# Dilated attention with the even tokens ahead of the odd ones, and value products of two pairs together

## What is computed

```
DIL_PATTERNS = ((128, 1), (512, 4), (2048, 16));  DIL_HEADS = 4;  HEAD_DIM = 64
for g, (w, r) in enumerate(DIL_PATTERNS):        # queries see keys at 0, +-r, ..., +-w/2
    o, lse = banded_attention(strided(q), strided(k), strided(v), w // (2 * r), 64, slopes[4g:4g+4], r)
wts = softmax(stack(lses), axis=0)               # over the three patterns of a head slot
out = sum(wts * outs)
```

## Time and profile before

| | us |
|---|---|
| median of 3 runs | 3207.03 (3205.33 to 3211.16) |
| profiled execution | 3205.56, span 3203.7 |
| TensorE busy / weight loads busy | 2553.3 (80%) / 1314.0 (41%) |
| VectorE, ScalarE, GpSimd busy | 1359.4, 881.3, 583.8 |
| DMA, mean over the span | 344 GB/s |

### The profile page before, as it was taken

The page is one execution under the profiler, slowest core; times in us unless marked ns, Lnnn a source line. Parts: engine busy times, 40 slices in busy tenths (PEclk is TensorE's granted clock), DMA queues, the critical chain, the costliest instruction groups (busy, mean ns, idle before and its releaser), DMA issues.

```text
span 3203.7 us, 31231 instructions
## 1 busy us (share of the span) xinstructions
PE 2553.3 (80%) x10802; PEld 1314.0 (41%) x10802; DVE 1359.4 (42%) x3265; ACT 881.3 (28%) x2329; POOL 583.8 (18%) x557
## 2 busy tenths in 40 slices
PE   8998766656999875666598887789897989977776
PEld 6775311111777521122165642245462544523222
DVE  0352100001144200000244767777867687677774
ACT  1231000000122101000123334455633475343433
POOL 0000000000000000000001334433434344344442
PEclk9999877787999887788899999999999999999999
DMA  7324899999533299999911899999999999999997
GB/s 287 127 103 155 341 428 428 428 428 428 209 121 132 105 422 427 428 427 428 423 74 63 340 422 421 421 421 402 419 422 421 410 414 408 420 421 422 421 421 317
DMA packets 120188, 1101.86 MB, mean 344 GB/s; under 512 B 13376, under 2 KB 17248, under 8 KB 20960
## 3 DMA queue, kind: packets, MB, share of 16 engines
q1 hardware_dynamic: 44576, 559.83, 42.1%
q0 software_dynamic: 73728, 536.90, 40.4%
q10 hardware_dynamic: 1728, 3.14, 0.3%
HBM read 1095.64 MB, written 4.19 MB: 343 GB/s over the span
## 4 chain that ended last, share of the span: by engine, by line
PE 42%; DMA 41%; DVE 9%; ACT 4%; issue 3%; POOL 0%; SPq 0%; DVEq 0%; ACTq 0%; POOLq 0%
PE ps L619 23%; DMA wbuf<-in_puv,ar 18%; PE ps L1173 9%; DMA wbuf<-in_w_expert_up 8%; DMA wbuf<-in_w_expert_down 8%; DMA wbuf<-in_w_expert_gate 4%; PE ps L847 4%; DVE ar L1841 3%; ACT ar L1890 2%; PE ps L719 2%; PE ps L623 2%; DMA wbuf<-in_w_mem_kv 2%; PE ps L705 1%; ACT L1890 1%; DMA Y<-in_mem 1%
## 5 line engine op out<-in xcount | busy, mean ns | idle before, releaser
L1173 PE MATMUL ps<-wbuf,ar 128*128 128x512 f32 x2048 | 968.2, 611 | 217.5 <-ACT ar L1890 217.3
L1841 DVE CUSTOM_DVE_ANT_0 ar<-wbuf,Y 128x1024 f32<-128x1024 f32 x512 | 627.4, 1225 | 334.8 <-DMA wbuf<-in_puv,ar 326.0
L847 PE MATMUL ps<-wbuf,ar 128*32 128x512 f32 x3072 | 495.0, 783 | 316.1 <-DMA wbuf<-in_w_expert_up 133.7
L2367 POOL DMA_INDIRECT wbuf<-in_puv,ar x512 | 558.7, 1091 | 842.5 <-PE ps L1173 804.8
L1173 PEld LDWEIGHTS ps<-wbuf,ar 128*128 128x128 f32 x2048 | 368.2, 192 | 769.8 <-issue 768.0
L619 PE MATMUL ps<-HT,wbuf 128*128 128x256 f32 (+2 forms) x2784 | 500.1, 339 | 12.5 <-DMA wbuf<-in_w_mem_kv 4.5
L619 PEld LDWEIGHTS ps<-HT,wbuf 128*128 128x128 f32 (+1 forms) x2784 | 439.2, 192 | 71.8 <-issue 14.1
L1890 ACT ACTIVATE ar<-ar 128x1 f32<-128x1 f32 (+2 forms) x1052 | 270.1, 257 | 657.6 <-DVE ar L1841 629.8
L847 PEld LDWEIGHTS ps<-wbuf,ar 128*32 128x32 f32 x3072 | 99.4, 127 | 699.0 <-issue 205.7
L2351 POOL TENSOR_TENSOR sm<-sm,co 128x1 f32<-128x1 f32 (+1 forms) x17 | 10.7, 632 | 1689.1 <-DVE sm L1208 1355.3
L1887 ACT COPY ar<-ps 128x512 f32<-128x512 f32 (+2 forms) x131 | 72.0, 550 | 620.4 <-PE ps L847 307.2
(11 more groups left out here) (139 smaller groups left out, 1506.9 us busy)
## 6 DMA issues: line engine op xcount, KB each, us to landing
wbuf<-in_w_expert_gate SPq DMA_DIRECT2D x64, 2048.0 KB, 26.3
wbuf<-in_w_expert_up SPq DMA_DIRECT2D x64, 2048.0 KB, 26.2
wbuf<-in_w_expert_down SPq DMA_DIRECT2D x64, 2048.0 KB, 27.3
wbuf<-in_w_in SPq DMA_DIRECT2D x22, 2048.0 KB, 11.2
wbuf<-in_peer_w_q SPq DMA_DIRECT2D x12, 2048.0 KB
wbuf<-in_w_o SPq DMA_DIRECT2D x6, 2048.0 KB, 7.1
wbuf<-in_b_w_in SPq DMA_DIRECT2D x6, 2048.0 KB
wbuf<-in_w_branch_b SPq DMA_DIRECT2D x4, 2048.0 KB, 15.3
```

The lines of the kernel that those rows point to most:

```text
L847: m = T.e.matmul(ps(jobs[n])[32 * k:32 * k + 32, :], lhs(c, k), v[:, k, 512 * n:512 * n + 512], start=(c == 0), stop=(c == 7), tile_positi ...
L1173: m = T.e.matmul(acc[n][:, :], DG[:, j % 4, :], rows_of(name)[:, 1024 + 512 * n:1536 + 512 * n], start=(j == 0), stop=(j == 127))
L1841: V.did(V.e.tensor_tensor_reduce(JK, rows_of(f"g{l}{i}.{j}")[:, 0:1024], Y[:, i, :], 1.0, 0.0, ALU.mult, ALU.add, DT[:, i, j:j + 1]), f"do ...
L2367: G.land(G.e.indirect_dma_start(out=rows_of(name), out_offset=None, in_=I["puv"], in_offset=bass.IndirectOffsetOnAxis(ap=IX[:, i, j:j + 1] ...
```

## The change

Queries and keys of the dilated attention are written with the 128 even tokens ahead of the 128 odd ones: the six jobs stream HT through a view `HE` whose innermost step is two elements (kind "E"), and the values' jobs load it as stationary operand with that step (kind "M", `proj_M`). A query block is now the tokens of one parity. The wide sub-heads see only keys of their own parity, so their scores have 128 columns each in place of 256; the local one keeps 256. A unit has 512 columns of scores, four transposes, and tables of 768 columns for 1152. Value products of a wide sub-head run per query block, over one block of keys. They are issued for two pairs at a time, after units 3 and 7, in turns on the two column halves. There are four buffers of transposed probabilities in place of two. The output is copied back to the order of tokens by a write with step two (`OAE`). Both wide sub-heads of a slot now lie on the other half of the rows than the local one.

```
+        OAE = OAT.rearrange("p c (t e) -> p c e t", e=2)
+        pb_dil = [arv(7680 + 1024 * k, 8704 + 1024 * k) for k in range(4)]
+        HE = HT[:, :, :].rearrange("p c (t e) -> p c e t", e=2)
 ...
-                    jobs.append((f"q{c}", j, "T", a, QK[:, c:c + 2, :], 0.125 if c < 6 else 1.0))
+                    jobs.append((f"q{c}", j, "E", a, QK[:, c:c + 2, :], 0.125 if c < 6 else 1.0))
-                jobs.append((f"va{i}", 3, "N", (i, 0, 512), VA[:, i, 0:512], 1.0))
+                jobs.append((f"va{i}", 3, "M", (i, 0, 512), VA[:, i, 0:512], 1.0))
 ...
         def dil_units(l):
+                local, *wide = heads = [4 * g + s for g in range(3)]
+                pv = [(f"m{l}.oa{s // 2}", 64 * (s % 2), 0, 256, k, 0, VA[:, k, 64 * local:64 * local + 64], k == 0, False)
+                      for k in range(2)]
+                for x, h in enumerate(wide):
+                    for i in range(2):
+                        pv.append((f"m{l}.oa{s // 2}", 64 * (s % 2), 128 * i, 128, 2 + x, i,
+                                   VA[:, i, 64 * h:64 * h + 64], False, (x, i) == (1, 1)))
+                pvs.append(pv)
 ...
-                        "scores": [(0, 0, 256, *qk[0]), (1, 0, 256, *qk[2]), (0, 256, 256, *qk[1])],
+                        "scores": [(0, 0, 256, q[0], kk[0]), (1, 0, 128, q[1], kk[1][:, qs]), (1, 128, 128, q[2], kk[2][:, qs])],
-                                  "parts": [(0, 0, 512, tab[:, 0:2, off:off + 256], 0),
-                                            (1, 0, 256, tab[:, 2, off:off + 256], 512)],
-                                  "cols": (0, 768), ...
+                                  "parts": [(0, 0, 256, tab[:, 256 * i:256 * i + 256], 0), (1, 0, 256, tab[:, 512:768], 256)],
+                                  "cols": (0, 512), ...
+                if s % 2:
+                    us[-1]["pv"] = [(*x, p) for both in zip(*pvs[s - 1:]) for x, p in zip(both, (s - 1, s))]
+                    us[-1]["close"] = [f"m{l}.oa{s // 2}"]
 ...
+            def proj_M(job, v, e, c0, n, *names):
+                b = take(job)
+                T.did(mm(b[:, 0:n], [(HE[:, c, e, :], v[:, c, c0:c0 + n]) for c in range(v.shape[1])]), job, *names)
 ...
-                                if u["pair"] > 1:
-                                    V.wait_ge(*at[f"{p}.pv{u['pair'] - 2}"])
+                                if u["before"] >= 0:
+                                    V.wait_ge(*at[f"{p}.pv{u['before']}"])
 ...
-                        copy(OAT[:, 0, :], ps(f"{p}oa0")[:, 0:256], f"{p}oa0.out")
+                        copy(OAE[:, 0, :, :], two(ps(f"{p}oa0")[:, 0:256]), f"{p}oa0.out")
 ...
-                u["tb"], u["pb"] = tbuf[k % len(tbuf)], pbuf[u["pair"] % 2]
+                u["tb"], u["pb"], u["before"] = tbuf[k % len(tbuf)], pbuf[u["pair"] % len(pbuf)], u["pair"] - len(pbuf)
 ...
-    order = [h ^ 1 if h // 4 == 1 else h for h in range(12)]
+    order = [h ^ 1 if h > 3 else h for h in range(12)]
```

More of the change, by code:

```diff
@@ L247, in dil_units @@
                     n = 2 * s + i
-                    tab = cbuf[:, s % 2, 0:1152].rearrange("p (g n) -> p g n", g=3)
+                    tab = cbuf[:, s % 2, 0:768]
                     us.append({
-                        "scores": [(0, 0, 256, *qk[0]), (1, 0, 256, *qk[2]), (0, 256, 256, *qk[1])],
+                        "scores": [(0, 0, 256, q[0], kk[0]), (1, 0, 128, q[1], kk[1][:, qs]), (1, 128, 128, q[2], kk[2][:, qs])],
                         "soft": [{"m": mx[:, n:n + 1], "nm": nm[:, n:n + 1], "den": den_dil[:, n:n + 1],
-                                  "parts": [(0, 0, 512, tab[:, 0:2, off:off + 256], 0),
-                                            (1, 0, 256, tab[:, 2, off:off + 256], 512)],
[L254 to L260, removed]
@@ new lines, in dil_units @@
+                                  "parts": [(0, 0, 256, tab[:, 256 * i:256 * i + 256], 0), (1, 0, 256, tab[:, 512:768], 256)],
+                                  "cols": (0, 512), "tab": f"m{l}.cd{s}", "over": f"m{l}.cd{s}.used" if i else None}],
+                        "m": mx[:, n:n + 1], "nm": nm[:, n:n + 1], "den": den_dil[:, n:n + 1],
+                        "blk": [128 * b for b in range(4)], "to": range(4), "nb": 4, "pair": s, "i": i, "ni": 2,
+                        "pv": [], "close": []})
@@ L652, in chunks @@
             def chunks(v, a, rhs):
-                return [(k, [(v[:, c, 128 * (a + k):128 * (a + k) + 128], rhs[:, c, :]) for c in range(v.shape[1])])
+                return [(k, [(v[:, c, 128 * (a + k):128 * (a + k) + 128], rhs[:, c]) for c in range(v.shape[1])])
                         for k in range(2)]
@@ L695, in attend @@
                     if j >= 0 and units[j]["pv"]:
[L696 to L700, removed]
+                        pairs = sorted({x[-1] for x in units[j]["pv"]})
+                        pb = {u["pair"]: u["pb"] for u in units[:j + 1]}
+                        for jj in range(j + 1):
+                            if units[jj]["pair"] in pairs:
+                                for c in range(0, len(units[jj]["blk"]), 4):
+                                    T.wait_ge(*at[f"{p}.t{jj}.{c}.out"])
+                        for job, po, c0, w, b, i0, v, start, stop, pair in units[j]["pv"]:
                             if job not in opened:
@@ L704, in attend @@
                             a = 128 * (units[j]["ni"] * b + i0)
-                            m = T.e.matmul(ps(job)[po:po + 64, c0:c0 + w], v, units[j]["pb"][:, a:a + w],
+                            m = T.e.matmul(ps(job)[po:po + 64, c0:c0 + w], v, pb[pair][:, a:a + w],
                                            start=start, stop=stop, tile_position=(0, po))
-                        T.did(m, f"{p}.pv{pair}", *units[j]["close"])
+                        T.did(m, *(f"{p}.pv{pair}" for pair in pairs), *units[j]["close"])
                         for job in units[j]["close"]:
@@ L725, in project @@
                     done = [f"m{l}.w{w}.used"] if n + 1 == len(jobs) or jobs[n + 1][1] != w else []
-                    if kind == "T":
-                        proj_T(f"m{l}.{job}", v, x, *done)
+                    if kind in "TE":
+                        proj_T(f"m{l}.{job}", v, x, *done, rhs=HE if kind == "E" else HT)
+                    elif kind == "M":
+                        proj_M(f"m{l}.{job}", v, *x, *done)
                     else:
@@ L1992, in mixer @@
                 A.wait_ge(*at[f"{p}oa1"])
-                copy(OAT[:, 1, :], ps(f"{p}oa1")[:, 0:256], f"{p}oa1.out")
+                copy(OAE[:, 1, :, :], two(ps(f"{p}oa1")[:, 0:256]), f"{p}oa1.out")
                 def heads_b(j):
@@ L2469, in _constants @@
     put("nhalf", -0.5)
[L2470 removed]
+    return {"cd": cd, "cw": cw.reshape(4, 128, 1536), "oh": oh, "co": co}
 def _arrays(inputs):
```

41 lines of the change are left out of this document (23 added, 18 removed).

## The result

The changed kernel took 3183.84 us (median of 4 runs, 3182.91 to 3187.18) against 3206.37 for the kernel before beside it (median of 4, 3205.33 to 3211.16): a ratio of 0.9931, 95% interval 0.9918 to 0.9944, 22.5 us less. The forecast was 3184.7. The profiled execution took 3187.18 us (span 3185.4), 18.4 us less than the profiled one of before.

The account below looks back on a forecast made before the run. TensorE was taken to pace the mixers, weight transfers the experts. Per layer 2.7 + 1.8 + 6.8 - 0.15 = 11.15 us, 22.3 for two, gave a median of 3184.7 us (forecast's own range 3180 to 3192; 8 in 10: 3179 to 3196).

Parts of the forecast that it names:

- scores: Dilated attention, each unit's score products: 1.06 us falls to 0.72, saving 2.7 us a layer (1.7 to 3.4).
- Transposes: Dilated attention: six per unit become four, saving 0.22 us for each of 8 units, 1.8 us a layer.
- Value products: Dilated attention: two pairs fall from 5.46 to 2.05 us by turns on column halves, saving 6.8 us a layer.
- Waits: Tail of the dilated attention: TensorE's idle gaps sum to 2.55 us against 2.38, losing 0.15 us a layer.
- the price of the stepped operand: Query and key projections streaming every second column: no cost taken; at half rate 41.7 us more a layer.
- my own sign: Projections: records above 0.22 us would prove the forecast wrong by rival (a) or (b).
- rival (a): Query and key projections: stepped stream is slow, gain eaten from 58 ns more a record, 3268 at half rate; chance 0.12.
- the weight loads of the values: Value projections loading the stepped operand as weights: no cost taken; at half rate 5.1 us a layer.
- The clock: Attention tail: layer 0 had lost 1.5 us to a lower granted clock; same loss taken once, 1.5 either way.
- rival d: Expert stages: the weight transfers do not start sooner, so the gain is hidden; chance 0.02.
- Rival (c): Value products: turns give nothing, 128-column products bound by weight loads; saving 2.7 a layer, total 3193; chance 0.04.
- (b): Value projections: only the stepped weight loads are slow, 5.1 us a layer, total 3195; chance 0.04.

Follow-up runs that it names:

- one-run step: Changed kernel, query and key projections reading 256 columns at step two in one run across two feature blocks (wrong values): 3184.59 us.
- the repeat: The changed kernel itself, unaltered, timed and profiled again beside its variants: 3185.06 us, ratio 0.9933 to the kernel before.
- evacuation variant: Changed kernel with queries and keys streamed without a step, the even/odd reordering done by the evacuations instead: 3182.63 us, ratio 0.9928.
- untwined order: Changed kernel with the first pair's value products all ahead of the second's, so not in turns on the column halves: 3192.24 us, ratio 0.9960.
- the step of four: Changed kernel with the query and key projections' streamed operand at a step of four columns, in four runs of 64: 3272.11 us.
- the best one: Changed kernel with the reordering moved into the evacuations and side work stretched into the attention's tail: 3174.11 us, ratio 0.9899 to the kernel before.

## Why the prediction was right

**Right in the mechanism of the attention; that the median came within 1 us is luck in part.** The forecast had 11.15 us a layer, from the attention alone. In the trace the attention gave 12.0 and 10.4, together 22.4, and the projections took 4.0 and 3.6 back. Term by term, a layer: scores 0.64 us a unit where I took 0.72, so 3.4 us for 2.7, the upper end of my bounds: the two products of 128 columns fit wholly beside the one of 256. Transposes 0.21 to 0.22 a unit (six in 0.71, four in 0.49 to 0.50, beside side work), as counted. Value products 1.89 us a group where I took 2.05: 7.1 for 6.8. Waits 2.60 us of idle gaps for 2.38 before, by the three places named (1.46, 0.32 and 0.82 for 1.5, 0.35 and 0.71). The sum of these is 12.1 a layer. The bounds of the recorded terms add up to 28 us for two layers at the top, where the prediction says 26; nothing hangs on it.

**The step that failed is the price of the stepped operand.** I took nothing, on the ground that a pass takes one column in two periods of the clock and so leaves the reads slack; it is 10.8 ns a record, 2.1 us a layer. By my own sign, records above 0.22 us, rival (a) came true in a mild form, at 0.228. The breakeven that I gave for it, 58 ns, stands five times higher, so the forecast survived. For the weight loads of the values, to take nothing was right: 0.196 for 0.190, beside passes of 0.217, and the stage still takes 20.8. Without the clock's part, the attention gives 12.0 a layer (58.3, as from 83.44 to 141.73 in the one-run step, for 70.3) and the step takes 2.1 of it, 19.8 in all; the loss of 1.5 us in layer 0's tail of the kernel before, if it isn't met again, makes it 21.3 for the 22.3 of the forecast. That run, which has the changed kernel's work and no slow stretch in its mixers, is 19.3 ahead at the start of the second block.

**The clock went against it, by more than I allowed.** I took the same 1.5 us once. In both profiles of the changed kernel the tail is slow in both layers, 1.5 to 1.7 us each, and both projections start slowly, 1.5 to 1.9 us. That is why the mixers' gain in the trace is 15.6 and not the forecast's 22.3. The profiled executions (3187.18, 3189.28) are the longest of their series, but the slow stretches are not shown to be the reason: the one-run step had none of them and took 3184.59, where 3187.2 less 6.6 would be 3180.6. So of the 22.5 us of the median, and of the 21.1 of the repeat (3206.14 less 3185.06), the rows account for about 15 in the profiled executions and for 19 to 21 without slow stretches. The rest comes from the identical second block and from the spread of the runs, and it happened to fill the gap to the forecast.

**The saving reached the end** (rival d): -8.6 at the first expert product is -9.0 when the next layer begins, and -15.6 in layer 1 is -14.7 behind its experts. The products themselves come later than forecast, at 324.65 for 322 and 15.6 earlier for 22, by the projections and the slow stretches. Rival (c) fell, in the run without turns: 3.24 us a group for 1.89. Products of 128 columns in turns cost 0.055 us a record (1.89 less 1.01 for the eight of 256, over 16), what the eight records of the earlier trace rows had as their lower reading. Of (b) nothing came.

## What to carry to other kernels

Two products that each fill half of the array's columns should be neighbours with different halves: it halved a group of value products here (2.74 us for 5.46), and deferring one pair until its partner is ready cost only more buffers (four for two) and a short wait (0.44 us). A reordering by parity cost 5% of an fp32 stream here at a step of two, and nothing that shows in the evacuation; a step of four doubled the stream. In a tail without side work, look at what the removed work had been covering, and split the last side jobs so that each step keeps one. Where single executions differ by as much as a change is worth, compare the start of the first stage behind it too, and not the total alone.

## What the runs showed of the hardware

The tail's gaps and the low clock: with gaps of 1.46, 0.32 and 0.82 us before the last value products, 9 of 12 tails had them in part or wholly at 1.2 GHz (the changed kernel 4 of 4, the evacuation variant 2 of 2, the untwined order 2 of 2, the step of four 1 of 2, the one-run step 0 of 2); with side work in the first two gaps, 0 of 4 (its own run and the best one). In the kernel before and in the one with value products together alone, whose first gap is 1.67, it was 1 of 2 each. Rows of the one-run step show that the same gaps need not do it: 1.89 us at the full clock (141.73 less 139.84). So the gaps go with the low clock in these traces, and what decides in a single execution stays open.

A streamed fp32 operand cost 217 ns for 256 columns without a step, 228 with a step of two, and 452 with a step of four (192 records in 41.68, 43.76 and 86.9 us). An evacuation of 512 fp32 columns that reads PSUM at a step of two took no longer than one without (0.59 to 0.60 us on ScalarE). Eight records of 256 and 16 of 128 columns, each on half of the array's columns, took 1.89 us in turns and 3.24 with one half's ahead of the other's, at 2.4 GHz in both.
